# Alternating the gate and up products of an inner feed-forward tile, in a fused two-layer encoder trunk

## What is computed

```python
def swiglu(h, w_in, w_out):
    gu = h @ w_in                                   # 1024 -> 2 x 2816
    gate, up = gu[..., :D_FF], gu[..., D_FF:]
    return (jax.nn.silu(gate) * up) @ w_out         # 2816 -> 1024

x = x + 0.5 * swiglu(rms_norm(x, g[0]), ffn_w_in[l, 0], ffn_w_out[l, 0])
x = x + s5_mixer(h, ...)       # layer 0; layer 1: mla_attention(...)
x = x + 0.5 * swiglu(rms_norm(x, g[2]), ffn_w_in[l, 1], ffn_w_out[l, 1])
```

## Time and profile before

| | |
|---|---|
| Span, first to last instruction, profiled execution | 1909.6 us |
| Other time of that execution | none given by the page beside the span |
| Runs: median (lowest to highest) | 1912.23 us (1907.93 to 1917.23) |
| TensorE matmul busy | 1834.8 us (96%), 8188 matmuls |
| VectorE, ScalarE, GpSimd busy | 970.3 us (51%), 594.9 us (31%), 262.9 us (14%) |
| Mean granted TensorE clock | 0.977 |

### The profile page before, as it was taken

One profiled execution on the slowest core, in us unless ns is written; L12 is line 12 of the kernel. 1 busy time (PEld: TensorE's weight loads), 2 busy tenths in 40 slices (PEclk: granted clock), 3 DMA queues, 4 the chain that ended last, 5 costly groups with the idle time before them and its releaser, 6 DMA issues.

```text
span 1909.6 us, 22284 instructions
## 1 busy us (share of the span) xinstructions
PE 1834.8 (96%) x8188; PEld 1490.0 (78%) x8188; DVE 970.3 (51%) x1274; ACT 594.9 (31%) x792; POOL 262.9 (14%) x178
## 2 busy tenths in 40 slices
PE   7888999997999999999999999999989999999997
PEld 5676788784788888888888888888866778888886
DVE  7889458734555544343346434333386354443333
ACT  5222123221133433332234333222235343332221
POOL 7456206300311400000010000001100100000010
PEclk8998999999899999999999999999999999999999
DMA  4244425556552232332232322322320232232221
GB/s 165 94 145 136 149 89 160 165 194 224 173 139 99 91 99 96 99 99 95 93 96 87 104 99 99 99 90 98 115 79 1 68 97 90 98 99 99 93 95 44
DMA packets 80477, 207.77 MB, mean 109 GB/s; under 512 B 24688, under 2 KB 35056, under 8 KB 78368
## 3 DMA queue, kind: packets, MB, share of 16 engines
q1 hardware_dynamic: 76160, 186.29, 30.9%
q0 software_dynamic: 3104, 18.55, 2.8%
q10 hardware_dynamic: 1152, 2.10, 0.3%
HBM read 183.84 MB, written 23.07 MB: 108 GB/s over the span
## 4 chain that ended last, share of the span: by engine, by line
PE 83%; DVE 8%; issue 3%; DMA 2%; ACT 2%; SPq 2%; POOL 0%; DVEq 0%; ACTq 0%; POOLq 0%
PE bank L1445 25%; PE bank L1447 25%; PE bank L1446 25%; DVE w_split L975 1%; SPq L424 1%; PE bank L1752 1%; PE bank L1754 1%; PE bank L1605 1%; PE bank L1771 1%; PE bank L1629 1%; PE bank L1636 1%; DMA s_ops<-k_window 1%; DMA s_u<-h_norm 1%; PE bank L1614 1%; DVE h_split L994 0%
## 5 line engine op out<-in xcount | busy, mean ns | idle before, releaser
L975 DVE TENSOR_TENSOR w_split<-w_raw,w_split 128x1024 fp32r<-128x1024 f32 x299 | 399.0, 1337 | 650.9 <-ACT w_split L644 648.1
L1445 PE MATMUL bank<-h_split,w_split 128*128 128x512 f32 x1512 | 596.0, 394 | 18.1 <-DVE gate L987 11.5
L1446 PE MATMUL bank<-h_split,w_split 128*128 128x512 f32 x1512 | 591.3, 391 | 0.0
L1447 PE MATMUL bank<-h_split,w_split 128*128 128x512 f32 x1512 | 591.2, 391 | 0.0
L644 ACT ACTIVATE w_split<-w_raw 128x1024 fp32r<-128x1024 f32 x299 | 315.3, 1058 | 657.4 <-PE bank L1447 653.6
L1445 PEld LDWEIGHTS bank<-h_split,w_split 128*128 128x128 f32 x1512 | 286.1, 189 | 82.2 <-DVE gate L987 11.9
L1445 PE MATMUL bank<-g_split,w_split 128*128 128x512 f32 (+1 forms) x854 | 332.3, 389 | 5.9 <-DVE g_split L989 3.9
L1446 PEld LDWEIGHTS bank<-h_split,w_split 128*128 128x128 f32 x1512 | 286.0, 189 | 60.0 <-issue 1.2
L1447 PEld LDWEIGHTS bank<-h_split,w_split 128*128 128x128 f32 x1512 | 285.7, 189 | 60.0
L1446 PE MATMUL bank<-g_split,w_split 128*128 128x512 f32 (+1 forms) x854 | 329.2, 386 | 0.0
L1447 PE MATMUL bank<-g_split,w_split 128*128 128x512 f32 (+1 forms) x854 | 329.1, 385 | 0.0
(11 more groups left out here) (260 smaller groups left out, 1162.0 us busy)
## 6 DMA issues: line engine op xcount, KB each, us to landing
w_raw<-wstream SPq DMA_DIRECT2D x299, 512.0 KB, 3.5
op_slots<-s_ops POOLq DMA_DIRECT2D x5, 2048.0 KB, 12.2
s_ops<-ops_out SPq DMA_DIRECT2D x8, 1024.0 KB, 4.6
op_slots<-s_ops SPq DMA_DIRECT2D x3, 2048.0 KB, 8.2
s_ops<-c_pow POOLq DMA_DIRECT2D x8, 512.0 KB, 5.8
s_ops<-k_window SPq DMA_DIRECT2D x64, 64.0 KB, 3.5
x_res<-xT SPq DMA_DIRECT2D x8, 256.0 KB, 8.0
bc_in<-bcd POOLq DMA_DIRECT2D x8, 256.0 KB, 5.8
```

The source lines that it names most:

```text
L975: tt(W[:, r, 1, :], RAW[:, r, :], W[:, r, 0, :].bitcast(F32), ALU.subtract).then_inc(s_lo, 1)
L1445: mm(bank, hi, x_hi, start=start, stop=True, skip_group_check=True)
L1446: mm(bank, hi, x_lo, start=False, stop=True, skip_group_check=True)
L1447: return mm(bank, lo, x_hi, start=False, stop=True, skip_group_check=True)
```

## The change

`in_tile` no longer runs the eight k-tiles of the gate pack and then those of the up pack. It waits for both packs at its start, takes gate and up matmul by matmul, and raises `s_used` twice at its end. The `between` of tile 10 in FFN0A1, which stood between the two halves, stands ahead of the tile. Number and kind of the matmuls, the banks and all other programs are as before. `pack(n)` waits until the low part of pack n is there.

```diff
             def in_tile(stage, f, par, base, src, i=None, between=None):
-                for q in range(2):
-                    if q and between:
-                        between()
-                    c = stage + f * 2 + q
-                    pack(c if i is None else i * 4 + c)
-                    column(c, in_banks(base, par)[q], src)
+                if between:
+                    between()
+                gate_pack, up_pack = (stage + f * 2 + q for q in range(2))
+                pack(up_pack if i is None else i * 4 + up_pack)
+                gate_bank, up_bank = in_banks(base, par)
+                for k in range(DT):
+                    g_hi, g_lo = tile(gate_pack, k)
+                    u_hi, u_lo = tile(up_pack, k)
+                    x_hi, x_lo = src[:, k, 0, :], src[:, k, 1, :]
+                    mm(gate_bank[:], g_hi, x_hi, start=k == 0, stop=True, skip_group_check=True)
+                    mm(up_bank[:], u_hi, x_hi, start=k == 0, stop=True, skip_group_check=True)
+                    mm(gate_bank[:], g_hi, x_lo, start=False, stop=True, skip_group_check=True)
+                    mm(up_bank[:], u_hi, x_lo, start=False, stop=True, skip_group_check=True)
+                    gate_last = mm(gate_bank[:], g_lo, x_hi, start=False, stop=True, skip_group_check=True)
+                    up_last = mm(up_bank[:], u_lo, x_hi, start=False, stop=True, skip_group_check=True)
+                gate_last.then_inc(s_used, 1)
+                up_last.then_inc(s_used, 1)
```

## The result

The change made the kernel slower. Four runs of it have a median of 1934.80 us (1933.72 to 1936.63), beside 1914.73 us (four runs) for the kernel before on the same chip. The ratio is 1.0122, with a 95% interval of 1.0101 to 1.0143. The profiled execution has a span of 1933.7 us, 24.1 more than before; the interval of the ratio is 19 to 27 us. The forecast was 1933 us, +21.1.

The account below looks back on a forecast made before the run. Long stages were taken as bound by TensorE's matmul spacing, FFN0A1 and FFN0A2 also by a VectorE, GpSimd, TensorE chain. Adding 15.9 and 5.2 us gave +21.1, a median of 1933 us, range 1926 to 1940.

Parts of the forecast that it names:

- The matmuls: All 90 tiles: 4320 matmuls at unchanged spacing, cost taken as 0, bounds -58 and +4 us.
- the row of a bank change in a first pair: In a first pair the bank changes every third matmul; that change costs 0.23 us, like any other.
- Plain stages: Stages without block products: the gate pack returns 5.44 us later, but the delay is hidden, also in `ffn_out` and GLU.
- all starts shifted by one number: Sign to look for: from FFN0B on, every start is later by one number near 21 us.
- FFN0A1: Stage +15.9 us: stalls ahead of block products, block product 3 ahead of tile 10, then `ffn_out` waiting for taps(3).
- FFN0A2: Stage +5.2 us: +4.7 at tile 9 from the block turns, some 0.5 for tile 10's gated product.
- Block product 5: 295.9 + 13.6 = 309.5: In FFN0A2, block product 5 starts 13.6 us after tile 3's end, at 309.5 instead of 306.92.
- forecast period of 27.9: Each turn with a block: 13.6 us to the block product, 3.4 for it, 10.9 for a tile.
- The sum: Whole kernel: 15.9 + 5.2 = 21.1 us on a span of 1909.6, giving 1930.7; median 1933.
- milder tail: Rival: steps put in a row at FFN0A1's tile 10 overlap; 10 us less, 1923 us, chance 0.10.
- heavier turns: Rival: the clock falls fully after each 2.7 us stall and tail low parts slow beside GpSimd; 1945 us, chance 0.12.

Follow-up runs that it names:

- run 1: Alternation only in GLU, FFN0B, FFN1A and FFN1B; FFN0A1 and FFN0A2 as in the kernel before. Ratio 1.0004 to the kernel before, span 1909.5 us.
- Run 5: Changed kernel with block product 3 in the middle of the alternated tile 10 of FFN0A1. Ratio 1.0102 to the kernel before, span 1931.4 us.
- run 7: Changed kernel with tables(3), taps(3) ahead of split(24) and b_bar(4) behind tile 10's gated product. Ratio 1.0055 to the kernel before, span 1918.6 us.
- Run 9: Changed kernel with tables(k) ahead of split(4i+8) on VectorE in FFN0A2. Ratio 1.0126 to the kernel before, span 1934.6 us.
- run 6: Changed kernel with tables(3), taps(3), b_bar(4) and ScalarE's operator copy ahead of split(24). Ratio 1.0091 to the kernel before, span 1932.0 us.
- run 8: Changed kernel with taps(k) and b_bar(k+1) ahead of split(4i+10) on VectorE in block turns. Ratio 1.0164 to the kernel before, span 1945.0 us.
- run 12: Kernel before with only b_bar(4) moved behind the gated product of tile 10. Ratio 0.9976, median 1907.09 us beside 1911.54.

## Why the prediction was right, point by point

**The matmuls.** 0 was taken, 0 measured (run 1). What held was the row of a bank change in a first pair. The granted clock of the alternated stretch is 1.00, the higher level. The rule of the Trainium skill ("TensorE: Matmul & The Clock Gate", section "A second HAM failure mode: psum-queue depth-cycling"), by which cycling through banks goes with idle times and a changing clock, is not borne out by the change of bank alone.

**Plain stages.** Hidden, as forecast, in FFN0B, FFN1B, GLU and all three `ffn_out` of 22 tiles. One place was missed: FFN1A, where split(158) stands ahead of the latent's reciprocal; +1.1, 1.0 of it ahead of tile 3. So the sign "all starts shifted by one number" from FFN0B on did not hold: there are two numbers, 22.96 and 24.05.

**FFN0A1.** The chain was right step by step: block products 1, 2 and 3 were forecast at 118.9, 149.1 and 177.1 and came at 119.81, 148.69 and 176.69, in the rows above; those of before are the earlier trace rows. `ffn_out` was forecast at 202.9 and came at 202.39. The stage cost 14.3 us (15.9 forecast). Of the difference 0.4 us were there at block product 3, and 0.8 came in the first 30 matmuls of `ffn_out`, which took 8.6 us and not 9.4. Run 5 shows what the block product's place is worth (4.9 us at `ffn_out`, 4.2 at FFN0A2's start), run 7 what the tail's order and b_bar(4)'s place are (12.5). They can't be added: together they are more than the stage lost.

**FFN0A2** was mis-sized: 9.4 us, 5.2 forecast. The term that failed is "Block product 5: 295.9 + 13.6 = 309.5". In the old scale it came at 327.15 - 14.5 = 312.7, 3.1 later. That step took b_bar to follow the end of tile 3 by 5.5 us; it took 8.8. The late pack of tile 2 had pushed tables(4) beside GpSimd's L526 and L528. VectorE after:

```profile
303.28 2.65 DVE L1049 TENSOR_TENSOR ops_out<-ops_out,gate 128x512 f32<-128x512 f32 x1
305.85 3.16 DVE L1050 TENSOR_TENSOR ops_out<-ops_out,up 128x512 f32<-128x512 f32 x1
```

The two take 0.7 each when GpSimd is still, as at 151.44 in the earlier trace rows. Run 9 took this away and block product 5 came 3.8 earlier. The turns behind came near the forecast period of 27.9, with 27.8 (327.15 to 354.98) and 28.7. The first did so by two errors that cancel: block product 5 took 2.7 us for 3.4, and the rest of the turn 25.1 for 24.5. What is left is clock: 4.1 and 4.2 us for block products 6 and 7, 3.4 forecast.

**The sum.** The span moved by 24.1, forecast 21.1; the 3.0 are 4.2 of FFN0A2, 1.1 of FFN1A and 0.2 ahead of the first tile, less 1.6 of FFN0A1 and less 0.9 that came in the S5 mixer and at GLU's first tile by themselves. The sum is better than its parts: two stages were missed in opposite directions, by 1.6 and 4.2 us, and the 0.9 owes nothing to the reasoning. That is luck. So is that the median missed by 1.8 us and the span by 3.0: the forecast put the median 2.6 us above the span, and in the changed kernel it is 1.1 above. Of the rivals, "milder tail" fell (the tail was as long as said), and "heavier turns" was partly true, through VectorE beside GpSimd rather than the clock alone.

## What to carry to other kernels

When two operands that were given back one by one are given back together, list what stands behind the later release on each in-order engine: here the cost wasn't in the tile but in table work of VectorE queued behind a split, and it was nothing where only splits stood there. Before moving work of VectorE or GpSimd earlier, look what the other does at the new time; three reorderings here (runs 6, 8 and 9) lost most or all of their gain where the two met, and the one that paid (runs 7 and 12) postponed GpSimd's powers.

## What the runs showed of the hardware

- VectorE's subtraction of 128x1024 from SBUF to SBUF takes 1.22 us alone, and up to 3.7 beside GpSimd's tensor operations: two in 2.36 us with GpSimd still (run 7), in 5.97 and 6.70 with it at work (runs 6 and 9). The 128x512 ones of the tables go from 0.69 to 2.65 and 3.16.
- In the traces this is a wait for GpSimd's instruction to end, and not a slower rate. In the kernel before an operation on 16x128, which takes 0.28 us elsewhere, took 2.39, from its start to just behind the end of GpSimd's (VectorE, then GpSimd):

```profile
180.95 2.39 DVE L1064 TENSOR_TENSOR k_window<-k_window,d_eye 16x128 f32<-16x128 f32 x1
180.94 2.25 POOL L521 TENSOR_TENSOR s_tmp<-bc_in,lam_pow_signed 128x1152 f32<-128x1152 f32 x1 [5.71 <-DMA bc_in<-bcd]
```

In the fourteen traces 189 of the packs' subtractions took 1.7 us or more. Each of them ends 1.08 to 1.09 us after a tensor operation of GpSimd has ended, which is nearly the 1.22 us that it takes alone. A step that reads a bank wasn't held in the same place: L985 of the kernel before took its 0.68 us at 190.16, in the middle of GpSimd's L532 (189.32 to 192.13). GpSimd's operations are lengthened in turn: L526 took 5.53 us beside the tables of the changed kernel (from 299.85), 2.94 for the same block before (from 285.36). So what such a split or table step pays is set by how long the instruction of GpSimd that is running still has to go, not by its own size.
- The same idle time of 3.5 us ahead of a block product was followed by a granted clock of 1.00 in one run (2.7 us to the next matmul, changed kernel) and of 0.50 in another (5.1 us, run 5). So repairs of 2 or 3 us in the stalls can't be read from one span.
- Alternating two banks matmul by matmul has the spacing of three on one bank, 0.227 us (changed kernel and run 1).
